# Another place in SBUF for the transposed activations' low part and for the four halves of the gate and up weight tiles

## What is computed

```python
for l in range(DEPTH):                       # DEPTH = 2, x is (1, 256, 1024)
    x = x + 0.5 * swiglu(rms_norm(x, ffn1_norm[l]), ffn1_w_gate[l], ffn1_w_up[l], ffn1_w_down[l])
    h = rms_norm(x, mix_norm[l])
    qa, ka, va, c_q, c_kv, k_r, g_a, g_b = jnp.split(h @ w_in[l], IN_OFFSETS, axis=-1)
    o_a = swa_attention(...)                 # sliding window, 8 heads
    o_b = mla_attention(...)                 # low-rank, 8 heads
    merged = sigmoid(g_a) * (o_a @ w_branch_a[l]) + sigmoid(g_b) * (o_b @ w_branch_b[l])
    x = x + merged @ w_out[l]
    x = x + 0.5 * swiglu(rms_norm(x, ffn2_norm[l]), ffn2_w_gate[l], ffn2_w_up[l], ffn2_w_down[l])

def swiglu(x, w_gate, w_up, w_down):         # 1024 -> 2816 -> 1024
    return (silu(x @ w_gate) * (x @ w_up)) @ w_down
```

## Time and profile before

| | |
|---|---|
| median of 3 runs | 1038.69 us (1038.49 to 1039.19) |
| profiled execution | 1039.14 us |
| its span, first to last instruction | 1037.3 us |
| PE busy | 1032.0 us, 5648 matmuls |
| PEld busy | 892.2 us, 5648 loads |
| DVE busy | 717.8 us |
| ACT busy | 586.5 us |
| POOL busy | 65.5 us |
| HBM | 185.98 MB read, 180 GB/s over the span |
| granted TensorE clock, mean | 0.999 |

### The profile page before, as it was taken

One profiled execution on the slowest core, in us unless ns is written; L12 is line 12 of the kernel. 1 busy time (PEld: TensorE's weight loads), 2 busy tenths in 40 slices (PEclk: granted clock), 3 DMA queues, 4 the chain that ended last, 5 costly groups with the idle time before them and its releaser, 6 DMA issues.

```text
span 1037.3 us, 15559 instructions
## 1 busy us (share of the span) xinstructions
PE 1032.0 (99%) x5648; PEld 892.2 (86%) x5648; DVE 717.8 (69%) x1132; ACT 586.5 (57%) x935; POOL 65.5 (6%) x71
## 2 busy tenths in 40 slices
PE   9999999999999999999999999999999999999998
PEld 7888888998888888888888888889988888888887
DVE  6766676668786876666687666666697868676665
ACT  7545454457864755454565455455688646454552
POOL 0052000122100000000000000001211000000000
PEclk9999999999999999999999999999999999999999
DMA  7665544455335555655545555634454346546551
GB/s 264 249 227 192 203 163 166 141 184 207 131 123 203 177 190 185 207 191 204 181 146 204 200 194 180 214 132 155 153 204 162 122 162 222 203 162 202 190 174 61
DMA packets 35269, 187.53 MB, mean 181 GB/s; under 512 B 4368, under 2 KB 4384, under 8 KB 20128
## 3 DMA queue, kind: packets, MB, share of 16 engines
q1 hardware_dynamic: 34992, 186.51, 51.6%
q0 software_dynamic: 240, 0.53, 0.2%
HBM read 185.98 MB, written 1.05 MB: 180 GB/s over the span
## 4 chain that ended last, share of the span: by engine, by line
PE 99%; DMA 1%; SPq 0%; DVE 0%; ACT 0%; issue 0%
PE ps L1369 96%; PE ps L1803 1%; PE ps L1393 1%; DMA w_raw<-in_w_ffn 1%; PE ps L1832 1%; PE ps L1868 0%; PE ps L1712 0%; PE ps L1704 0%; PE ps L1414 0%; DVE x_cols L999 0%; ACT w_hi L554 0%; SPq L318 0%; SPq L317 0%
## 5 line engine op out<-in xcount | busy, mean ns | idle before, releaser
L1369 PE MATMUL ps<-hT,w_hi 128*128 128x512 f32 x1408 | 341.2, 391 | 0.9 <-ACT w_hi L554 0.9
L1369 PEld LDWEIGHTS ps<-hT,w_hi 128*128 128x128 f32 x1408 | 258.9, 188 | 51.4 <-ACT w_hi L554 1.1
L884 DVE TENSOR_TENSOR w_lo<-w_raw,w_hi 128x2048 fp32r<-128x2048 f32 x82 | 188.0, 2292 | 87.4 <-ACT w_hi L549 87.4
L1369 PEld LDWEIGHTS ps<-hT,w_lo 128*128 128x128 f32 x1408 | 176.7, 188 | 7.5
L1369 PE MATMUL ps<-hT,w_lo 128*128 128x256 f32 x1408 | 178.3, 279 | 0.0
L1369 PE MATMUL ps<-w_hi,hT 128*128 128x512 f32 (+2 forms) x576 | 173.5, 376 | 0.0
L549 ACT ACTIVATE w_hi<-w_raw 128x2048 fp32r<-128x2048 f32 x85 | 161.9, 1905 | 13.6 <-PE ps L1369 13.2
L1369 PE MATMUL ps<-w_lo,aTh 128*128 128x512 f32 x352 | 137.1, 390 | 0.0
L1369 PE MATMUL ps<-w_hi,aTl 128*128 128x512 f32 x352 | 137.0, 389 | 0.0
L1369 PE MATMUL ps<-w_hi,aTh 128*128 128x512 f32 x352 | 136.8, 390 | 0.0
L578 ACT ACTIVATE S<-ps 128x256 f32<-128x256 f32 x88 | 33.7, 383 | 155.4 <-PE ps L1369 155.4
(11 more groups left out here) (168 smaller groups left out, 956.9 us busy)
## 6 DMA issues: line engine op xcount, KB each, us to landing
w_raw<-in_w_ffn SPq DMA_DIRECT2D x85, 1024.0 KB, 5.0
w_raw<-in_w_ffn SPq DMA_DIRECT2D x90, 512.0 KB, 5.8
w_raw<-in_w_gate SPq DMA_DIRECT2D x16, 1024.0 KB, 4.9
w_raw<-in_w_proj SPq DMA_DIRECT2D x16, 592.0 KB, 4.3
w_raw<-in_w_branch SPq DMA_DIRECT2D x8, 1024.0 KB, 4.9
w_raw<-in_w_out SPq DMA_DIRECT2D x8, 1024.0 KB, 4.9
w_raw<-in_w_uq SPq DMA_DIRECT2D x4, 384.0 KB, 3.1
w_raw<-in_w_ffn SPq DMA_DIRECT2D x4, 256.0 KB, 6.2
```

The lines of the kernel that those rows point to most:

```text
L884: dve.tensor_tensor(wl_gu[b], raw_gu[b], wh_gu[b].bitcast(F32), ALU.subtract).then_inc(lo_gu.sem, 1)
L1369: return pe.matmul(dst, w, m, start=start, stop=stop, skip_group_check=True)
```

## The change

The low part of the transposed activations is moved 8 elements (32 bytes) away from the high part, and the distance from chunk to chunk goes from 512 to 576 elements. `w_hi` gets slots of 2176 elements like `w_lo` (now both `PART_SLOT`). In both, the gate half and the up half of a gate/up tile lie at places of their own: in `w_hi` 0 and 8 elements beyond where they would follow one another in slot 0, 112 and 120 in slot 1; in `w_lo` 108 and 118 in slot 0, 100 and 119 in slot 1. A gate/up tile in `w_hi` or `w_lo` thus has two runs of 1024 elements, and the copy and the subtraction that make it address it as [2, 1024]; the high matmul's moving operand has two runs of 256. All other edits follow from this addressing. Nothing is added or taken away in instructions, waits or DMAs.

```diff
-LO_SHIFT = 120
-LO_SLOT = GU_COLS + 128
+HI_AT, LO_AT = ((0, 8), (112, 120)), ((108, 118), (100, 119))
+HT_GAP = 8
+PART_SLOT = GU_COLS + 128
...
-        w_hi = sb("w_hi", [P, MIX_SLOTS * GU_COLS], F32R)
-        w_lo = sb("w_lo", [P, MIX_SLOTS * LO_SLOT], F32R)
-        raw_gu, wh_gu = ([w[:, i * GU_COLS:(i + 1) * GU_COLS] for i in range(2)] for w in (w_raw, w_hi))
-        wl_gu = [w_lo[:, i * LO_SLOT + LO_SHIFT:i * LO_SLOT + LO_SHIFT + GU_COLS] for i in range(2)]
...
+        w_hi = sb("w_hi", [P, MIX_SLOTS * PART_SLOT], F32R)
+        w_lo = sb("w_lo", [P, MIX_SLOTS * PART_SLOT], F32R)
+        raw_gu = [w_raw[:, i * GU_COLS:(i + 1) * GU_COLS] for i in range(2)]
+
+        def halves(w, i, gate_at, up_at):
+
+            step = KC * P + up_at - gate_at
+            a = i * PART_SLOT + gate_at
+            return w[:, a:a + 2 * step].rearrange("p (s n) -> p s n", s=2)[:, :, 0:KC * P]
+
+        def cols_of(w, c, n):
+
+            return w[:, c // (KC * P), c % (KC * P):c % (KC * P) + n]
+
+        wh_gu, wl_gu = ([halves(w, i, *at) for i, at in enumerate(places)] for w, places in ((w_hi, HI_AT), (w_lo, LO_AT)))
...
+        mix_hi, mix_lo = ([w[:, i * PART_SLOT:i * PART_SLOT + GU_COLS] for i in range(MIX_SLOTS)] for w in (w_hi, w_lo))
+        hT = sb("hT", [P, KC, 2 * SEQ + 64], F32R)[:, :, 0:2 * (SEQ + HT_GAP)].rearrange("p k (s n) -> p k s n", s=2)[:, :, :, 0:SEQ]
...
-                    act.activation(wh_gu[b], raw_gu[b], ACT.Copy).then_inc(hi_gu.sem, 1)
+                    act.activation(wh_gu[b], raw_gu[b].rearrange("p (s n) -> p s n", s=2), ACT.Copy).then_inc(hi_gu.sem, 1)
...
-                    dve.tensor_tensor(wl_gu[b], raw_gu[b], wh_gu[b].bitcast(F32), ALU.subtract).then_inc(lo_gu.sem, 1)
+                    dve.tensor_tensor(wl_gu[b], raw_gu[b].rearrange("p (s n) -> p s n", s=2), wh_gu[b].bitcast(F32), ALU.subtract).then_inc(lo_gu.sem, 1)
...
-                    return mm(ps[:, bank, :], hi, hT[:, k, :, :].rearrange("p s n -> p (s n)"), first, last)
+                    return mm(ps[:, bank, :].rearrange("p (s n) -> p s n", s=2), hi, hT[:, k, :, :], first, last)
...
-                            high(2 * b + s, wh_gu[b][:, c:c + P], k, k == 0)
+                            high(2 * b + s, cols_of(wh_gu[b], c, P), k, k == 0)
...
-                            ins = low(2 * b + s, wl_gu[b][:, c:c + P], k, k == KC - 1)
+                            ins = low(2 * b + s, cols_of(wl_gu[b], c, P), k, k == KC - 1)
```

More of the change, by code:

```diff
@@ L548, in split_gu @@
                         act.wait_ge(gu_used.sem, gu_used.at(n // 2 - 1, FFN2_0 + FB - 2 + e))
[L549 removed]
+                    act.activation(wh_gu[b], raw_gu[b].rearrange("p (s n) -> p s n", s=2), ACT.Copy).then_inc(hi_gu.sem, 1)
                 def start_high(i):
                     act.wait_ge(start_in[i].sem, 16)
[L554 removed]
+                    act.activation(cols_of(wh_gu[0], start_cols(i).start, HALF), raw_gu[0][:, start_cols(i)], ACT.Copy)\
                        .then_inc(start_hi.sem if i < 3 else hi_gu.sem, 1)
@@ L561, in third_high @@
                     act.wait_ge(gu_used.sem, gu_used.at(0, 0))
-                    act.activation(wh_gu[0][:, part], third_raw[:, part], ACT.Copy)\
+                    act.activation(cols_of(wh_gu[0], part.start, KC * P), third_raw[:, part], ACT.Copy)\
                        .then_inc((third_hi, hi_gu)[half].sem, 1)
@@ L715, in _ @@
                         act.wait_ge(landed.sem, 16)
-                        act.activation(wh_gu[1][:, part], raw_gu[1][:, part], ACT.Copy).then_inc(sig.sem, 1)
+                        act.activation(cols_of(wh_gu[1], part.start, KC * P), raw_gu[1][:, part], ACT.Copy).then_inc(sig.sem, 1)
                     act.wait_ge(ss_clear.sem, 1)
@@ L1452, in gate_up_low_first @@
                             c = (s * KC + k) * P
-                            low(2 * b + s, wl_gu[b][:, c:c + P], k, False, k == 0)
+                            low(2 * b + s, cols_of(wl_gu[b], c, P), k, False, k == 0)
                     for s, sig in enumerate((gate_ps, gu_used)):
@@ L1456, in gate_up_low_first @@
                             c = (s * KC + k) * P
-                            ins = high(2 * b + s, wh_gu[b][:, c:c + P], k, False, k == KC - 1)
+                            ins = high(2 * b + s, cols_of(wh_gu[b], c, P), k, False, k == KC - 1)
                         ins.then_inc(sig.sem, 1)
@@ L1484, in gate_up_first @@
                                 c = s * KC * P
-                                low(s, wl_gu[0][:, c:c + P], 0, False, True)
+                                low(s, cols_of(wl_gu[0], c, P), 0, False, True)
                         pe.wait_ge(ht_lo.sem, ht_lo.at(l, 2 * w * KC + k))
@@ L1488, in gate_up_first @@
                             c = (s * KC + k) * P
-                            high(s, wh_gu[0][:, c:c + P], k, False)
+                            high(s, cols_of(wh_gu[0], c, P), k, False)
                         if k == 0:
@@ L1493, in gate_up_first @@
                             c = (s * KC + k) * P
-                            ins = low(s, wl_gu[0][:, c:c + P], k, k == KC - 1)
+                            ins = low(s, cols_of(wl_gu[0], c, P), k, k == KC - 1)
                             if k == KC - 1:
@@ L1508, in start_high_four @@
                         c = (s * KC + k) * P
-                        high(s, wh_gu[0][:, c:c + P], k, k == 0)
+                        high(s, cols_of(wh_gu[0], c, P), k, k == 0)
                 def start_low_four(s, half):
@@ L1551, in gate_up_second @@
                             c = (s * KC + k) * P
-                            high(2 + s, wh_gu[1][:, c:c + P], k, k == 0)
+                            high(2 + s, cols_of(wh_gu[1], c, P), k, k == 0)
                             if l + w == 0 and s == 1 and k == 4:
@@ L1558, in gate_up_second @@
                             c = (s * KC + k) * P
-                            ins = low(2 + s, wl_gu[1][:, c:c + P], k, k == KC - 1)
+                            ins = low(2 + s, cols_of(wl_gu[1], c, P), k, k == KC - 1)
                         ins.then_inc(sig.sem, 1)
```

18 lines of the change are left out of this document (8 added, 10 removed).

## The result

The changed kernel takes 1051.26 us (1050.86 to 1052.05, 4 runs) beside 1038.91 us for the kernel before on the same chip: a ratio of 1.0122, interval 1.011 to 1.0134. The forecast was 1032.1 us, faster, with a range that ends at 1044.5. It is wrong in sign and outside the range.

What follows compares the result with a forecast made beforehand. The prediction took TensorE's matmul pitch to bound the kernel, with almost no waits. Gains of 4.6 + 1.6 + 0.4 = 6.6 us took the median of 1038.69 to 1032.1 us, range 1019.0 to 1044.5.

Steps and rivals of the forecast that it cites:

- the odd block's slower high matmuls behind off-phase lows: Feed-forward loop: 228.7 ns against 226.9 in the even block, read as TensorE's pitch reacting to operand places.
- part 5: ScalarE and VectorE: splits addressed as two runs add nothing; subtraction and copy keep 2292 and 1905 ns.
- Both signs of being wrong: The high matmuls' pitch moving by more than 2 ns in either direction, or the mixing stage moving.
- Part 1: 1408 low gate/up matmuls: the 3.3 ns above 113.3 goes, 4.6 us gained; worst end 4.6 us lost.
- 113.3 is what the 512-column rows imply per column: Low matmuls: half of the 512-column pitch of 226.7 ns, taken as reachable from 116.6 ns.
- Part 2: 1408 high matmuls, two-run moving operand and new weight places: pitch 227.8 to 226.7 ns, 1.6 us gained.
- C: High matmuls: the skipped 32 bytes restart the stream, 233.2 ns each, 7.6 us lost, 1046.3 us; chance 0.13.
- Part 3: Down products directly behind low matmuls, 13 places: 0.03 us excess each, 0.4 us gained if the low matmuls' excess goes.
- Part 4: Mixing sub-layer and down products: cost 0, bounds 1.0 us either way for 288 mixing matmuls with low activations stationary.
- 39 ns to spare: Mixing: a 188 ns load of low activations under a 226.7 ns matmul, so their 32-byte move was costed at 0.
- A: The forecast itself: the excess over the common pitch goes, 1032.1 us; chance 0.38.
- B: High matmuls: the gap also lowers them to 220.0 ns, 9.4 us more gained, 1022.7 us; chance 0.27.

Runs made afterwards that it cites:

- the turns: TensorE alone on constant data in the loop's matmul order, low tiles at each place 0 to 63: 16.362 (19, 45) to 16.669 us (51) per turn.
- the probe: TensorE alone on constant data, 53 streams of 48 matmuls at different stationary and moving places: 226.7 ns (512 columns, difference 0), 113.3 ns (256 columns, 80).
- 80: Kernel before with the low gate/up tiles at 80 elements in place of 120: 1040.03 us, ratio 1.0012, low matmuls at 117.8 ns.

## Why the prediction was wrong

- **What bounds the kernel**: right. PE is busy for 99 to 100% of the span, TensorE waits for 1.3 us, and the time moved by pitch alone. That the pitch reacts to places was right too, in part by luck: one of its two signs, the odd block's slower high matmuls behind off-phase lows, stays at 3.65 us when the lows are on phase. The parts costed at nothing on the other engines (part 5) were right. Both signs of being wrong that the prediction named came: the high matmul's pitch in the loop went from 227.8 to 231.7 ns, and the mixing stage moved.
- **Part 1, low tiles, 4.6 us gained**: wrong, 3.3 us lost. The step that failed is "113.3 is what the 512-column rows imply per column": the price of a distance was carried over from 512 to 256 columns, where it isn't the same. The rows held one fact only, that lows at 480 bytes run at 116.6 ns. I read the excess as the cost of being off phase, and took any new offsets as a cure. On phase the lows run at 119.7 ns (1042.8 us). The offset of 120 was a gain already. Nearly that, 113.8 to 114.0, exists in the turns, but only at 3 of 64 places (19, 22 and 45), none of which is among the changed kernel's. The worst end that I gave, 4.6 us lost, held the truth.
- **Part 2, high matmuls, 1.6 us gained**: wrong, 5.3 us lost. The two 512-column rows that I leaned on, down products and mixing, had a difference of 0 modulo 256 bytes, and the change leaves that. The prediction had written this down and then costed the moved matmuls by the unmoved ones. The rival for a loss (C) had a fair size (7.6) and a wrong mechanism: two runs are free, the place of the second isn't.
- **Part 3, transients, 0.4 us gained**: wrong. The twelve matmuls of a down product behind lows, 2.75 us by the prediction, take 2.77 to 2.78 us in the changed kernel, and 2.75 to 2.76 with the lows on phase; the three down groups lost 1.1 us of busy time. Being off phase wasn't what made the transients. They do depend on the places (3.626 to 3.690 us for the odd block's highs), by no rule that the runs show.
- **Part 4, mixing, 0 with 1.0 us either way**: wrong, 3.6 us lost. The step was "39 ns to spare". A load with 39 ns to spare still delays the stream beside it: the matmul with the low weights went from 227 to 240 ns, which is more than any steady stream of the probe has (233.4). The bound came from the low matmuls' 3.3 ns, which is not the price of a place but what was left of it at a good place.
- **The chances**: 0.65 for faster, on an argument that never said which differences are good. Two cases that rest on the same unproven sign, A and B, should have been one, with a mirror image of equal weight: places picked without a rule for them are more often worse, as the 64 turns show (six better than the place of before, 55 worse).

What stays open: why the period is 256 bytes, why a difference of 0 is best for 512 columns and nearly worst for 256, why one off-phase load among three costs its neighbour 13 ns where a stream of them costs 6.6 each, and what makes the rhythms. The runs show only that these need nothing but TensorE at work, and that they follow the distance between its two operands.

## What to carry to other kernels

Where TensorE is the bound and its weight loads run beside its streams, the place of the stationary tile relative to the moving one, modulo 256 bytes, is a parameter: the best place found gained 0.4% here, the changed kernel's places lost 1.2%. Keep everything at a multiple of 256 bytes for 512-column streams, and scan for 256-column ones. Scan with TensorE alone and the real order of matmuls: it gave the loop turn of this kernel to 0.01 us, while streams of one form alone missed (80). Let the scan repeat the order until two turns agree. An excess over a round figure in a trace doesn't say in which direction the next change will move it.

## What the runs showed of the hardware

- The pitch of float32r matmuls depends on the distance between the chunk being loaded and the chunk that streams, with a period of 64 elements (256 bytes): 226.7 to 233.4 ns in steady streams of 512 columns, 113.3 to 120.9 ns for 256 among the places tried. A single 512-column matmul beside a load 32 bytes off took 240 ns in the mixing sub-layer.
- A moving operand in two runs costs nothing by itself (226.7 ns with gap 0 and gap 64).
- TensorE keeps a rhythm across instructions: at the same places (80) a stream ran at 113.3 or 117.8 ns depending on what ran before, moving only the high tiles slowed the low matmuls by 1.5 us, and the same turn run twice (high tiles at 60) had its lows at 3.780 and then 3.641 us.
- ScalarE, VectorE and DMA traffic beside it (44 to 324 GB/s in the stretches of a turn) left the loop turn unchanged to 0.01 us.
